# Half of the prompt's change of order (high parts) given to GpSimd through a second spare

## The reference, cut to what matters

```python
h = rms_norm(x, ln_g) * (1.0 + scale) + shift
# A: differential attention, B: 2-D neighbourhood attention with a relative bias,
# C: dilated sliding-window attention; all three project the same h
qkv_a, qkv_b, qkv_c = h @ w_in[:, A], h @ w_in[:, B], h @ w_in[:, C]
...
merged = sum(sigmoid(h @ w_g[i]) * ((y_i * silu(h @ w_z[i])) @ w_br[i]) for i in range(3))
x = x + gate * (merged @ w_out)
```

## Time and profile before

| what | us |
|---|---|
| median of 3 runs | 2329.15 |
| lowest and highest | 2327.76, 2329.62 |
| the profiled execution's own time | 2327.98 |
| its span | 2326.2 |
| TensorE busy | 2289.1 (98%) |
| VectorE busy | 1647.1 (71%) |
| ScalarE busy | 1122.8 (48%) |
| GpSimd busy | 58.6 (3%) |

### The profile page before, as it was taken

One profiled execution on the slowest core, in us unless ns is written; L12 is line 12 of the kernel. 1 busy time (PEld: TensorE's weight loads), 2 busy tenths in 40 slices (PEclk: granted clock), 3 DMA queues, 4 the chain that ended last, 5 costly groups with the idle time before them and its releaser, 6 DMA issues.

```text
span 2326.2 us, 42010 instructions
## 1 busy us (share of the span) xinstructions
PE 2289.1 (98%) x15370; PEld 2137.4 (92%) x15370; DVE 1647.1 (71%) x4547; ACT 1122.8 (48%) x3077; POOL 58.6 (3%) x103
## 2 busy tenths in 40 slices
PE   7999999999999999999999999999999999999999
PEld 5888889999998999999888899899999989999998
DVE  7887677777765666676578867777877656576772
ACT  5666565444444443344356765744444354343440
POOL 0010110000000000000001002100000000000000
PEclk9999999999999999999999999999999999999999
DMA  7221411111113243221521021121111223333223
GB/s 284 96 76 53 126 63 57 62 57 60 56 48 119 71 129 119 92 91 63 175 81 35 34 84 42 59 83 60 56 52 41 82 85 114 105 113 98 87 91 118
DMA packets 74556, 198.72 MB, mean 85 GB/s; under 512 B 10864, under 2 KB 31984, under 8 KB 71408
## 3 DMA queue, kind: packets, MB, share of 16 engines
q1 hardware_dynamic: 59232, 170.29, 21.5%
q10 hardware_dynamic: 15120, 25.74, 3.1%
HBM read 175.02 MB, written 18.87 MB: 83 GB/s over the span
## 4 chain that ended last, share of the span: by engine, by line
PE 88%; DVE 6%; ACT 3%; issue 2%; DMA 1%; SPq 0%; DVEq 0%; ACTq 0%
PE ps_proj L1046 54%; PE ps_score L1090 10%; PE ps_pt L1090 8%; PE ps_score L1223 2%; PE ps_pt L1239 2%; PE ps_pv L1275 2%; PE ps_score L1207 1%; PE ps_pv L1256 1%; PE ps_tr L1290 1%; DMA y_part<-parked 1%; PE ps_tr L1291 1%; PE ps_pv L1269 1%; PE ps_pt L1282 1%; ACT act_hi L1500 1%; DVE top L2123 1%
## 5 line engine op out<-in xcount | busy, mean ns | idle before, releaser
L1046 PE MATMUL ps_proj<-w_hi,act_hi 128*128 128x384 f32 x1824 | 634.0, 348 | 2.2 <-ACT act_hi L1500 1.3
L1046 PE MATMUL ps_proj<-w_hi,act_lo 128*128 128x384 f32 x1824 | 613.0, 336 | 0.0
L1046 PE MATMUL ps_proj<-w_lo,act_hi 128*128 128x384 f32 x1824 | 612.7, 336 | 0.0
L1046 PEld LDWEIGHTS ps_proj<-w_hi,act_hi 128*128 128x128 f32 x1824 | 343.2, 188 | 7.3 <-ACT act_hi L1500 4.9
L1046 PEld LDWEIGHTS ps_proj<-w_lo,act_hi 128*128 128x128 f32 x1824 | 343.9, 189 | 0.0
L1046 PEld LDWEIGHTS ps_proj<-w_hi,act_lo 128*128 128x128 f32 x1824 | 343.0, 188 | 0.0
L2052 DVE TENSOR_REDUCE ssq<-square 128x2 f32<-128x256 f32 (+1 forms) x228 | 95.5, 419 | 204.9 <-ACT square L1598 204.1
L1598 ACT ACTIVATE square<-ps_proj 128x256 f32<-128x256 f32 x228 | 87.7, 385 | 263.9 <-PE ps_proj L1046 263.5
L2416 DVE TENSOR_TENSOR w_lo<-w_raw,w_hi 128x1536 fp32r<-128x1536 f32 (+3 forms) x105 | 169.2, 1612 | 23.4 <-ACT w_hi L1424 22.7
L1424 ACT ACTIVATE w_hi<-w_raw 128x1536 fp32r<-128x1536 f32 (+2 forms) x104 | 144.2, 1386 | 44.1 <-DMA w_raw<-in_w 25.0
L2326 DVE TENSOR_TENSOR s_lo<-s_raw,s_hi 128x512 fp32r<-128x512 f32 x224 | 150.9, 686 | 2.1 <-ACT s_hi L1756 0.4
(11 more groups left out here) (261 smaller groups left out, 5057.7 us busy)
## 6 DMA issues: line engine op xcount, KB each, us to landing
w_raw<-in_w SPq DMA_DIRECT2D x80, 768.0 KB, 5.7
s_raw<-in_w_gate SPq DMA_DIRECT2D x96, 256.0 KB, 3.2
w_ada<-in_w_mod SPq DMA_DIRECT2D x11, 1536.0 KB, 6.8
w_raw<-in_w SPq DMA_DIRECT2D x24, 512.0 KB, 3.8
wb_raw<-in_w_branch SPq DMA_DIRECT2D x24, 512.0 KB, 3.7
first_ada<-in_w_first SPq DMA_DIRECT2D x8, 1024.0 KB, 12.9
w<-in_w_gate SPq DMA_DIRECT2D x32, 256.0 KB, 3.7
parked<-y_t ACTq DMA_DIRECT2D x4, 1536.0 KB, 5.3
```

The lines of the kernel that those rows point to most:

```text
L1046: op = pe.matmul(out, sta[s](k), mov[m](k), start=(k == 0 and n == 0), stop=(k == chunks - 1 and n == 2))
```

## The change

GpSimd takes part in the moves of the high parts. Moves 5, 6 and 7 (slots 5 to 7 to slots 4 to 6) and move 8 (the spare to slot 7) are GpSimd's. Move 4 (slot 4 to slot 3) is cut in two: GpSimd copies slot 4 in the new order to a second spare (another piece of `yz_hi`, where `mod_row` lies at other times), and ScalarE copies that one, contiguous, to slot 3. ScalarE keeps moves 0 to 3. GpSimd starts after parts 0 and 1 of the bias of head 3 and ahead of parts 2 and 3; each of its copies waits for the one before. ScalarE's copy of move 4 stands at the end of unit ("q", l, "B", 3, 0, 5), and it does no move at the start of unit ("q", l, "C", 0, 0, 0). TensorE waits for ScalarE's count up to slot 3 and for GpSimd's from slot 4 on. VectorE's moves of the low parts stay as they are.

```diff
+LAST_MIDDLE = max((u for u in LAYER_UNITS[0] if u[0] == "a" and AT[u] < AT["q", 0, "C", 0, 0, 0]), key=AT.get, default=None)
...
+HI_MOVES = {("B", 3, 0, 4): range(0, 4), ("B", 3, 0, 5): range(4, 5)}
+POOL_MOVES = range(4, KC + 1)
 MOVES = {("B", 3, 0, 4): range(0, 4), ("B", 3, 0, 5): range(4, 7), ("C", 0, 0, 0): range(7, KC + 1)}
...
-        hi_moved = tally("hi_moved", [(l, n) for l in layers for n in range(KC + 1)])
+        hi_moved = tally("hi_moved", [(l, n) for l in layers for n in range(5)])
+        pool_moved = tally("pool_moved", [(l, n) for l in layers for n in POOL_MOVES])
...
+                    if part == 2 and h == HEADS - 1:
+                        for n in POOL_MOVES:
+                            move(l, n)
                     if part == 2:
                         pool.wait_ge(*rel_s_in.at((l, h)))
...
+            def move(l, n):
+
+                if n == POOL_MOVES[0]:
+                    pool.wait_ge(*proj_ready.at(("q", l, "B", 3, 0, 3)))
+                    if l == 0:
+                        pool.wait_ge(*turned_t.at(("t", LAST_MIDDLE)))
+                else:
+                    pool.wait_ge(*pool_moved.at((l, n - 1)))
+                if n == KC:
+                    pool.wait_ge(*hi_moved.at((l, 0)))
+                dst, src = move_views(act_hi, yz_hi[:, 0, 0:SEQ], n)
+                if n == POOL_MOVES[0]:
+                    dst = yz_hi[:, 3, 0:SEQ].rearrange("p (r k x) -> p r k x", r=4, k=8)
+                pool.tensor_copy(dst, src).then_inc(*pool_moved.inc((l, n)))
...
                     if u == ("q", l, "C", 0, 0, 0) and k < KC - 1:
-                        pe.wait_ge(*hi_moved.at((l, k + 2)))
+                        pe.wait_ge(*(hi_moved if k < 3 else pool_moved).at((l, k + 2)))
                         pe.wait_ge(*lo_moved.at((l, k + 2)))
...
                 dst, src = move_views(act_hi, yz_hi[:, 0, 0:SEQ], n)
+                if n == 4:
+
+                    act.wait_ge(*pool_moved.at((l, 4)))
+                    dst, src = act_hi[:, 3, 0:SEQ], yz_hi[:, 3, 0:SEQ]
                 act.activation(dst, src, ACT.Copy).then_inc(*hi_moved.inc((l, n)))
...
-                    for i in MOVES[u[2:]]:
+                    for i in HI_MOVES.get(u[2:], ()):
                         move_high(l, i)
...
-                    dve.wait_ge(*hi_moved.at((l, KC)))
+                    dve.wait_ge(*hi_moved.at((l, 4)))
+                    dve.wait_ge(*pool_moved.at((l, KC)))
                     dve.wait_ge(*lo_moved.at((l, KC)))
```

## The result

| kernel | median us | against the kernel before |
|---|---|---|
| before, runs on the same chip | 2328.58 | |
| changed | 2333.27 | ratio 1.0018, 95% interval 1.0012 to 1.0023 |

The change costs 4.7 us (2.8 to 5.4 by the interval). It was forecast at 5.4 us; the median of 2333.27 lies 1.2 us under the 2334.5 that was forecast, within the range and inside the forecast's own case. It is just short of the 0.2% from which on the forecast counts a change as slower: that had a chance of 0.50, and what came, within 0.2%, one of 0.47. The profiled execution has a span of 2330.9 us.

A forecast was written before the change was run, and what follows sets the result against it. TensorE, busy 98%, bounds the kernel; in this stretch ScalarE's moves delay it. Per layer 4.0 lost, 1.8 gained, 0.5 for the clock: 2 x (4.0 - 1.8 + 0.5) = 5.4 us, median 2334.5, range 2326.5 to 2341.

The forecast's parts named there:

- the forecast's own case: GpSimd copies of 0.9 to 1.5 us, held against VectorE: 2331 to 2338 us, chance 0.50.
- What bounds the stretch, and the gain of 1.8 us per layer: Second half of the moves: ScalarE is late; relieved, the next unit starts at 347.2 instead of 349.0, 1.8 us per layer.
- The copies are held and hold: From 333.1 on, GpSimd's copies and VectorE's low moves hold each other up for whole instructions, taking turns.
- Rival 1: VectorE's copies are not held, only `w_lo` waits 0.4 us: -2.8 us, 2326.4; chance 0.20.
- rival 4: The change does nothing: GpSimd is late and TensorE waits for its slots, needing copies over 2 us; chance 0.03.
- The copy's duration: GpSimd's 128x512 copy with large read step: 1.2 us, between 0.6 (memset) and 1.6 (bias addition); contiguous 0.8 us.
- Rival 2: Held, but cheap copies of 0.6 to 0.8 us: VectorE 1.8 to 2.5 us late, 2329 to 2331; chance 0.15.
- What VectorE pays: Before the reduction of 338.7: `w_lo` waits 0.4 us, three copies precede move 3 (3.6 us), so 4.0 us late.
- The sign "`w_lo` lengthened": In the changed profile, `w_lo` and the first half's low moves would be lengthened, the latter from 0.6-0.7 to about 1.8 us.
- Where the loss lands: VectorE's lateness reaches TensorE in full: its 342.60 becomes 346.6, with the whole second half 4.0 us later.
- The clock: Longer TensorE pauses make a drop to 1.2 GHz likelier in the last chunks: 0.5 us added per layer.
- waits on L2232, 0.7 us apart: Sign for the second half: TensorE would wait on VectorE's low moves, 0.7 us apart, and no longer on L1500.

The follow-up runs named there:

- the filled kernel: The changed kernel plus 31 filler matmuls of 256 columns, read by nobody, in TensorE's pauses: 2331.58 us, ratio 1.0013 to the kernel before; again 2331.45, 1.0015.
- the last version: Against the kernel before, GpSimd makes two copies in VectorE's free windows and VectorE puts one spare back: 2326.29 us, again 2326.18, ratio 0.9991 both times.

## Why the prediction was right, and where it was not

- **What bounds the stretch, and the gain of 1.8 us per layer**: right. Without the copies the stretches were 1.90 and 1.69 us shorter.
- **The copies are held and hold**: right, and the main step. Rival 1 (not held, 2326.4) falls with the first low moves, 1.67 and 1.42 us instead of 0.6 to 0.7; rival 4 with TensorE, which never waited for a GpSimd slot.
- **The copy's duration**: 1.2 us was forecast from a bracket of 0.6 to 1.6; unheld it takes 1.14 us, contiguous 0.70 (0.8 forecast). Rival 2 needed copies of 0.6 to 0.8 us. Leaning towards the bias addition because of the large read step held up: with the step the copy takes 1.14 us, without it 0.70.
- **What VectorE pays**: 4.0 us forecast, 3.26 and 3.17 measured. This term was mis-sized, in how the turns fall. The prediction had `w_lo` wait 0.4 us and three copies ahead of low move 3. In fact the operation that meets the first copies is the scaling L2167, which stands between `qk` and `w_lo` and which the prediction didn't look at; it pays 2.13 - 0.62 = 1.5 us for two copies. Then `w_lo`, back to back behind it, keeps GpSimd's third copy out for 1.75 us, which costs VectorE nothing. All five copies do get in ahead of move 3, but they cost less than their length: the first had run for 0.45 us before the scaling came, the third waited for `w_lo`, and the fifth, contiguous, cost move 2 between 0.1 and 0.2 us. The sign "`w_lo` lengthened" didn't show, since `w_lo` always got in first.
- **Where the loss lands**: right. The transposes of 342.60 came 3.2 us later, VectorE's lateness in full. TensorE was idle before the unit's first chunk behind `gained` (2.25 us) and before the transposes (1.73 us).
- **The clock**: 0.5 us per layer forecast, because in the earlier trace rows a drop cost nothing. Measured, against the filled kernel, 1.25 and 1.09 us in the stretch (1.49 and 0.93 with the changed kernel's first execution), at the lower level in both layers. The term had the right sign and half the size: the slots that paced the second half at 1.2 us before, and had hidden the drop of the earlier trace rows, were just what the change took away. The kernel with copies that nobody waits for kept those slots, had the clock at 0.50 as well, and paid nothing for it. Beside half rate the low moves of 0.7 us no longer set the pace; TensorE does, to the end of the unit.
- **The sum**: 2 x (3.2 - 1.8 + 1.2) = 5.2 us from the measured terms, 5.3 in the stretches, 5.4 forecast. Two errors, 0.8 too much for VectorE and 0.7 too little for the clock, cancel: that the total came this close is luck, its terms were not that good.
- **The second half**: "waits on L2232, 0.7 us apart" didn't show; at half rate the slots were always there first.

## What to carry to other kernels

Before work is given to an idle GpSimd, list what VectorE does in the window where it will run, operation by operation, and count one GpSimd instruction as a wait for each that it meets, tiny ones and scalings with a per-partition factor too. A relief that pays 1.8 us for one engine bought 3.2 us of holding and then 1.2 us of clock; the same idea with two copies in windows where VectorE read the accumulators or nothing cost nothing. And when a pause is made longer, ask what used to hide the half-rate matmuls behind it.

## What the runs showed of the hardware

- The scaling of 256 elements by a per-partition factor, 0.62 us for a pair, took 2.13 us beside GpSimd's copies and 0.97 beside its memsets. `w_lo`, which has two inputs, took 1.74 us beside memsets, unheld.
- A GpSimd copy of 128x512 took 1.14 us with a read step of 32 elements and 0.70 contiguous.
- A code packet of 0.02 MB in the DMA queues went with 3.7 to 3.9 us instead of 2.8 to 3.0 for a DMA of 192 KB where it fell beside it, in five of five cases. Thirty-one more instructions on TensorE moved it there, 480 us behind where they stand. Two kernels that differ by some instructions can so differ by 1 to 2 us at places that the edit doesn't touch.
- In one execution of the last version the clock fell to 0.50 in layer 0 after a pause of 1.09 us; in the other it stayed at 1.00 after one of 1.15 us (layer 1). What decides it, the pause alone doesn't tell.
